# Rotated heads: swapping the halves by transfers inside SBUF in place of permutation matmuls

## The reference

```
def rope(x, pos):
    ...
    x1, x2 = xf[..., :half], xf[..., half:]
    return jnp.concatenate([x1 * cos - x2 * sin, x2 * cos + x1 * sin], axis=-1).astype(x.dtype)
```

## Time and profile before

| | |
|---|---|
| time, median of 3 runs | 2386.9 us (2386.45 to 2389.05) |
| time of the profiled execution | 2386.32 us |
| its span | 2384.5 us |
| granted TensorE clock, mean | 0.994 of full speed |
| TensorE matmul busy | 2313.1 us (97%) |
| VectorE busy | 1319.5 us (55%) |
| ScalarE busy | 954.6 us (40%) |
| GpSimd busy | 416.1 us (17%) |
| moved by DMA | 203.77 MB, mean 85 GB/s |

### The profile page before, as it was taken

One profiled execution on the slowest core, in us unless ns is written; L12 is line 12 of the kernel. 1 busy time (PEld: TensorE's weight loads), 2 busy tenths in 40 slices (PEclk: granted clock), 3 DMA queues, 4 the chain that ended last, 5 costly groups with the idle time before them and its releaser, 6 DMA issues.

```text
span 2384.5 us, 29941 instructions
## 1 busy us (share of the span) xinstructions
PE 2313.1 (97%) x11494; PEld 1821.1 (76%) x11494; DVE 1319.5 (55%) x1687; ACT 954.6 (40%) x1394; POOL 416.1 (17%) x410
## 2 busy tenths in 40 slices
PE   9999999999999989999999899999999999999997
PEld 7775668888888668888887668888888658888886
DVE  6447647664547567664548865433347685433334
ACT  4327853443323473443324353322225772323222
POOL 0003423110004134110004033200121004211000
PEclk9999999999999999999999999999999999999999
DMA  5220002222223112222223112222323201322221
GB/s 187 106 71 36 2 2 98 95 96 97 89 106 115 36 37 93 102 90 103 88 104 129 59 56 88 104 88 106 106 88 115 71 19 71 106 100 94 88 106 71
DMA packets 31493, 203.77 MB, mean 85 GB/s; under 512 B 4261, under 2 KB 5289, under 8 KB 7721
## 3 DMA queue, kind: packets, MB, share of 16 engines
q1 hardware_dynamic: 30104, 199.37, 23.5%
q10 hardware_dynamic: 1296, 3.15, 0.4%
HBM read 200.41 MB, written 2.10 MB: 85 GB/s over the span
## 4 chain that ended last, share of the span: by engine, by line
PE 84%; DVE 8%; ACT 6%; issue 2%; DMA 0%; POOL 0%; DVEq 0%; ACTq 0%; SPq 0%
PE D L586 73%; PE X L691 3%; PE D L705 3%; PE D L713 2%; DVE w_lo L1667 1%; ACT prob L1324 1%; ACT w_hi L1120 1%; ACT prob_t L1120 1%; PE X L697 1%; DVE xg L1695 1%; DVE prob L1985 1%; DVE rstd_b L1712 1%; ACT mid L1120 0%; PE X L816 0%; DVE conv_out L1805 0%
## 5 line engine op out<-in xcount | busy, mean ns | idle before, releaser
L586 PE MATMUL D<-xg,w_hi 128*128 128x512 f32 x3184 | 988.6, 392 | 6.5 <-DVE w_lo L1667 6.2
L586 PE MATMUL D<-mid,w_hi 128*128 128x512 f32 x2308 | 713.7, 390 | 16.7 <-DVE mid L1667 6.9
L586 PEld LDWEIGHTS D<-xg,w_hi 128*128 128x128 f32 x3184 | 596.3, 188 | 139.7 <-issue 9.0
L586 PE MATMUL D<-xg,w_lo 128*128 128x512 f32 x1592 | 619.7, 389 | 0.0
L1667 DVE TENSOR_TENSOR w_lo<-w_raw,w_hi 128x2048 fp32r<-128x2048 f32 (+2 forms) x210 | 458.7, 2186 | 282.0 <-ACT w_hi L1120 281.8
L1120 ACT ACTIVATE w_hi<-w_raw 128x2048 fp32r<-128x2048 f32 (+2 forms) x210 | 355.9, 1695 | 586.9 <-PE D L586 583.0
L586 PEld LDWEIGHTS D<-mid,w_hi 128*128 128x128 f32 x2308 | 433.1, 188 | 111.1 <-issue 12.1
L586 PE MATMUL D<-mid,w_lo 128*128 128x512 f32 x1154 | 449.8, 390 | 0.0
L586 PEld LDWEIGHTS D<-xg,w_lo 128*128 128x128 f32 x1592 | 298.9, 188 | 62.9
L1720 DVE TENSOR_TENSOR h<-D,h 128x1024 f32 (+1 forms) x71 | 86.9, 1224 | 354.0 <-PE D L586 353.9
L586 PEld LDWEIGHTS D<-mid,w_lo 128*128 128x128 f32 x1154 | 217.0, 188 | 45.5
(11 more groups left out here) (277 smaller groups left out, 1784.4 us busy)
## 6 DMA issues: line engine op xcount, KB each, us to landing
w_raw<-in_weights SPq DMA_DIRECT2D x184, 1024.0 KB, 4.8
h<-in_x SPq DMA_DIRECT2D x4, 512.0 KB, 7.0
out_y<-h SPq DMA_DIRECT2D x4, 512.0 KB, 2.7
w_raw<-in_weights SPq DMA_DIRECT2D x2, 512.0 KB, 6.6
inv_cnt<-in_inv_cnt ACTq DMA_DIRECT2D x1, 1024.0 KB, 5.0
cos<-in_cos ACTq DMA_DIRECT2D x3, 256.0 KB, 5.0
sin<-in_sin ACTq DMA_DIRECT2D x3, 256.0 KB, 5.4
vec<-in_vec SPq DMA_DIRECT2D x1, 272.0 KB, 2.8
```

The lines of the kernel that those rows point to most:

```text
L586: last = nc.tensor.matmul(out, w[a], x[b], start=start and k == 0, stop=stop and k == 2)
```

## The change

In nsa, swa and even the query and key tiles are no longer multiplied by the permutation. ScalarE, right behind its copy of a tile pair out of PSUM, waits until that copy is done and issues four transfers from SBUF to SBUF, each of 32 partitions, which write the swapped halves into `rope_t` (queries), `kt[:, 1]` (nsa keys, for the second pair after a wait until the first is rotated) or the new `ks2` (keys of swa and even). VectorE waits for 64 increments of `q_swapped` or `k_swapped`, and multiplies the swapped copy in place by sin; the minus sign has moved to the table of sines. `swap`, `query_swap`, `last_swap`, `swap_keys` and `swap_queries` are gone from TensorE, as are its waits that belonged to them; `key_swap` is left with the transposes of the values and is called `turn_values`. The compressed keys of nsa keep their matmul with the permutation.

```diff
+def swapped_rows():
+
+    return [(slice(r, r + HD // 2), slice(r + s, r + s + HD // 2))
+            for at in (0, HD) for r, s in ((at, HD // 2), (at + HD // 2, -(HD // 2)))]
...
+             ("ks2", [P, SEQ], F32),
...
-                    if s == 1 and kind in SINK0:
-
-                        last_swap(u)
...
-                            pe.wait_ge(q_half, late_before[l] + 1)
+                            pe.wait_ge(d_free[u % 2], u // 2 + 1)
...
-            def swap(u, out):
-
-                pe.wait_ge(d_free[u % 2], u // 2 + 1)
-                for j in range(2):
-                    last = nc.tensor.matmul(out[:, j, :], perm[:, :], zq[:, j, :], start=True, stop=True)
-                last.then_inc(q_rot, 1)
...
-            def key_swap(u, pair):
+            def turn_values(u, pair):
                 pe.wait_ge(d_free[u % 2], u // 2 + 1)
-                nc.tensor.matmul(X[:, 2 * pair, :], perm[:, :], kz2[:, :], start=True, stop=True).then_inc(k_rot, 1)
                 for t in range(QT):
                     last = nc.tensor.transpose(X[:, 2 * pair + 1, span(t)], vz2[:, span(t)], ident[:, :])
                 last.then_inc(v_turned, 1)
...
-                        if (z, k) == (0, 0):
-                            swap(u - 1, X[:, 0:2, :])
...
-                def swap_keys(n):
-                    u = at["k"] + n
-                    pe.wait_ge(d_free[u % 2], u // 2 + 1)
-                    for t in range(2):
-                        last = nc.tensor.matmul(X[:, 2 * n + t, :], perm[:, :], kz[:, n, t, :], start=True, stop=True)
-                    last.then_inc(k_rot, 1)
...
-                swap(at["q"], X[:, 0:2, :])
...
-                project(at["k"] + 1, x_norm, middle=lambda: swap_keys(0))
-                compressed_hidden(0, at["cmp_w1"], lambda: swap_keys(1))
+                project(at["k"] + 1, x_norm)
+                compressed_hidden(0, at["cmp_w1"], None)
...
-                project(at["q"] + 2, x_norm, middle=query_swap(at["q"] + 1, 0))
+                project(at["q"] + 2, x_norm)
                 project(at["gate"], x_norm, outs=1)
-                swap(at["q"] + 2, X[:, 0:2, :])
...
-                def first_middle():
-                    token_roots(l)
-                    swap(q, X[:, 0:2, :])
-
                 project(q, x_norm, norm=l)
-                project(q + 1, x_norm, middle=first_middle)
-                project(q + 2, x_norm, middle=query_swap(q + 1, 1))
+                project(q + 1, x_norm, middle=lambda: token_roots(l))
+                project(q + 2, x_norm)
                 pe.wait_ge(kv_low, 4)
-                project(at["kv"], x_kv, middle=query_swap(q + 2, 0))
-                pe.wait_ge(q_ready, qpairs_before[l] + 2)
-                project(at["q_last"], x_norm, middle=lambda: key_swap(at["kv"], 1))
+                project(at["kv"], x_kv)
+                project(at["q_last"], x_norm, middle=lambda: turn_values(at["kv"], 1))
...
-                def swap_queries():
-                    pe.wait_ge(d_free[at["pool"] % 2], at["pool"] // 2 + 1)
-                    swap(at["q"], X[:, 0:2, :])
...
-                project(at["q"], x_norm, middle=lambda: key_swap(at["kv"], 0))
+                project(at["q"], x_norm, middle=lambda: turn_values(at["kv"], 0))
...
-                project(at["q_last"], x_norm, middle=swap_queries)
+                project(at["q_last"], x_norm)
...
+                act.wait_ge(d_free[s], u // 2 + 1)
+                for out, of in swapped_rows():
+                    act.dma_start(rope_t[out, :, :], zq[of, :, :]).then_inc(q_swapped, 16)
...
+                act.wait_ge(d_free[s], u // 2 + 1)
+                for out, of in swapped_rows():
+                    act.dma_start(ks2[out, :], kz2[of, :]).then_inc(k_swapped, 16)
...
+                    if n:
+                        act.wait_ge(k_ready, krope_before[l] + n)
+                    act.wait_ge(d_free[s], (u + n) // 2 + 1)
+                    for out, of in swapped_rows():
+                        act.dma_start(kt[out, 1, :, :], kz[of, n, :, :]).then_inc(k_swapped, 16)
...
-                dve.wait_ge(q_rot, qpairs_before[l] + n + 1)
+                dve.wait_ge(q_swapped, 64 * (qpairs_before[l] + n + 1))
                 nc.vector.scalar_tensor_tensor(zq[:, :, :], zq[:, :, :], scale, cos[:, :].unsqueeze(1).to_broadcast(two),
                                                ALU.mult, ALU.mult)
-                link(nc.vector.scalar_tensor_tensor(rope_t[:, :, :], X[:, 2 * pair:2 * pair + 2, :], scale,
+                link(nc.vector.scalar_tensor_tensor(rope_t[:, :, :], rope_t[:, :, :], scale,
...
-                    dve.wait_ge(q_rot, qpairs_before[l] + n + 1)
-                    nc.vector.scalar_tensor_tensor(rope_t[:, :, :], D[:, 2 * (u % 2):2 * (u % 2) + 2, :], scale,
+                    dve.wait_ge(q_swapped, 64 * (qpairs_before[l] + n + 1))
+                    nc.vector.scalar_tensor_tensor(rope_t[:, :, :], rope_t[:, :, :], scale,
...
-            def key_rotary(l, bank):
-
-                dve.wait_ge(k_rot, krope_before[l] + 1)
-                nc.vector.tensor_tensor(rope_t[:, 0, :], kz2[:, :], cos[:, :], ALU.mult)
-                link(nc.vector.tensor_tensor(rope_t[:, 1, :], X[:, bank, :], sin[:, :], ALU.mult))
+            def key_rotary(l):
+
+                dve.wait_ge(k_swapped, 64 * (krope_before[l] + 1))
+                nc.vector.tensor_tensor(kz2[:, :], kz2[:, :], cos[:, :], ALU.mult)
+                link(nc.vector.tensor_tensor(ks2[:, :], ks2[:, :], sin[:, :], ALU.mult))
                 for g in range(2):
                     for side in range(2):
-                        ins = nc.vector.tensor_tensor(kd2[rows_of(side), g, :], rope_t[rows_of(g), 0, :],
-                                                      rope_t[rows_of(g), 1, :], ALU.add)
+                        ins = nc.vector.tensor_tensor(kd2[rows_of(side), g, :], kz2[rows_of(g), :],
+                                                      ks2[rows_of(g), :], ALU.add)
...
-                    dve.wait_ge(k_rot, krope_before[l] + n + 1)
+                    dve.wait_ge(k_swapped, 64 * (krope_before[l] + n + 1))
                     two = [P, 2, SEQ]
                     nc.vector.tensor_tensor(kt[:, 0], kz[:, n], cos[:, :].unsqueeze(1).to_broadcast(two), ALU.mult)
-                    link(nc.vector.tensor_tensor(kt[:, 1], X[:, 2 * n:2 * n + 2, :],
+                    link(nc.vector.tensor_tensor(kt[:, 1], kt[:, 1],
...
+    c["sin"] = np.where((np.arange(P) % HD < HD // 2)[:, None], -c["sin"], c["sin"])
```

More of the change, by code:

```diff
@@ L220, in build_program @@
         kdup, vall, kz, c_prob_t = (second[x] for x in ("kdup", "vall", "kz", "c_prob_t"))
-        kd2, va2, pool_s, pool_u, inv_cnt, kz2, vz2 = (
-            second[x] for x in ("kd2", "va2", "pool_s", "pool_u", "inv_cnt", "kz2", "vz2"))
+        kd2, va2, pool_s, pool_u, inv_cnt, kz2, ks2, vz2 = (
+            second[x] for x in ("kd2", "va2", "pool_s", "pool_u", "inv_cnt", "kz2", "ks2", "vz2"))
         QUERY = {"nsa": mids["q_all"], "swa": mids["q_all"], "even": mids["q_even"]}
@@ L349, in build_program @@
         out_done = sem("out_done")
[L351 removed]
+        k_swapped = sem("k_swapped")
         k_ready = sem("k_ready")
         v_ready = sem("v_ready")
[L354 removed]
+        q_swapped = sem("q_swapped")
         q_ready = sem("q_ready")
@@ L810, in attend @@
                         times_values(kind, units[n], a0 + n, n % per == per - 1)
-            def swap(u, out):
-                pe.wait_ge(d_free[u % 2], u // 2 + 1)
-                for j in range(2):
-                    last = nc.tensor.matmul(out[:, j, :], perm[:, :], zq[:, j, :], start=True, stop=True)
-                last.then_inc(q_rot, 1)
-            def query_swap(u, pair):
-                return lambda: swap(u, X[:, 2 * pair:2 * pair + 2, :])
-            def last_swap(u):
-                swap(u, D[:, 2 * (u % 2):2 * (u % 2) + 2, :])
             def attention_ends(kind, l):
@@ L889, in compressed_hidden @@
                     last.then_inc(w_used, 1)
-                    if z == 0:
+                    if z == 0 and middle is not None:
                         middle()
@@ L2119, in nsa @@
                     split_low(q + n)
-                query_rotary("nsa", l, 0, 0)
+                query_rotary("nsa", l, 0)
                 dve.wait_ge(cmp_rot, 1)
@@ L2131, in nsa @@
                 split_low(at["gate"])
-                query_rotary("nsa", l, 1, 0)
+                query_rotary("nsa", l, 1)
                 split_low(at["q_last"])
-                query_rotary("nsa", l, 2, 0)
+                query_rotary("nsa", l, 2)
                 split_low(at["v"])
@@ L2138, in nsa @@
                 split_low(at["v"] + 1)
-                query_rotary("nsa", l, 3, 0)
+                query_rotary("nsa", l, 3)
                 compressed_max(0)
@@ L2157, in swa @@
                     split_low((q + 2, at["kv"], at["q_last"])[n])
-                    query_rotary("swa", l, n, n % 2)
```

(3 more changed lines are left out.)

8 lines of the change are left out of this document (3 added, 5 removed).

## The result

| | before | after |
|---|---|---|
| time, median of 6 runs each, same chip | 2388.04 us (2386.45 to 2392.01) | 2399.07 us (2394.03 to 2404.97) |
| time of the profiled execution | 2386.32 us | 2399.79 us |
| its span | 2384.5 us | 2398.0 us |

The ratio after to before is 1.0043, 95% interval 1.0027 to 1.006. The forecast was 2384.7 us in a range of 2376 to 2393, so it was on the wrong side of no change, and the time lies beyond the range.

The account below looks back on a forecast made before the run. The prediction took TensorE, 84% of the span on the chain, as the bound. Layer changes of -5.8 (nsa), +2.35 (swa) and +1.2 us (even) sum to -2.2 on the median 2386.9, giving 2384.7 us, range 2376 to 2393.

Parts of the forecast that it names:

- the kv unit: swa's key/value projection: TensorE arrives 3.4 us earlier but waits for late weights; both swaps lost, +1.15 us.
- the late pair: Last query pair, rotated inside the attention's third step in swa: VectorE's first step starts later, +1.95 us.
- The landing term: At each swap: transfers land 2.7 us after issue, so swapped data is there 4.0 us after the copy's end.
- The transfers with slack: nsa query pairs 0, 1 and 3: later weights stay ready before TensorE needs them, so each gives 1.7 us.
- The first term: TensorE: removing 52 swap matmuls of 0.43 us takes off 22.4 us, nearly 1% if nothing else moved.
- 0.4 each, so 1.6 us: ScalarE behind each copy: four transfer issues of 0.4 us, making ScalarE 1.8 us later with wait and lost overlap.
- The second: the clock: TensorE's half speed behind pauses: nsa keys regain 2.1 us, swa's key/value projection loses 1.8; 2.74 us pauses keep full clock.
- Rival 4: Every new TensorE pause halves the clock: +2.1 us in nsa, about +1 in each attention, 2389 us; chance 0.12.
- Rival 1: ScalarE does not stand still: issues run beside its next instruction, weights never late; -12 us, 2375; chance 0.12.
- Rival 2: Transfers land late, at 5.4 us, delaying VectorE in both attentions and key rotaries; +7.6 us, 2392; chance 0.14.
- Rival 3: The four pieces of each swap serialize wholly, 10.8 us from first issue; +34 us, 2419; chance 0.04.

Follow-up runs that it names:

- nsa keys back: The changed kernel with nsa's two key swaps done by matmuls again, all other swaps by ScalarE's transfers; ratio 1.0013 to the kernel before.
- swa pairs 0, 1 back: The changed kernel with swa's first two query pairs swapped by matmuls again, everything else by ScalarE's transfers; ratio 1.0007 to the kernel before.
- the filler alone: The changed kernel plus products of bf16 zeros in TensorE's pauses in nsa and ahead of swa's key/value unit; 2393.88 us, ratio 1.0018 to the kernel before.
- issues on SyncE: The changed kernel with its 56 transfers issued by SyncE between weight loads instead of by ScalarE; 2385.91 us, ratio 0.9967 to the kernel before.
- mix 1: The kernel before with ScalarE-issued transfers only for nsa query pairs 0, 1, 3, swa pair 2 and swa's keys; 2379.19 us, ratio 0.9954.

## Why the prediction was wrong

**Read rightly.** Every place of loss was named: the nsa keys, the weights of nsa's last query unit, the kv unit, the late pair, even's last query unit. The landing term held: the late step can begin 4.2 us after the copy's end (817.34 + 1.02 to 822.55), forecast 4.0. The transfers with slack gave what was forecast: nsa's first three query copies stand at 105.06, 118.78 and 130.99 us where they stood at 102.30, 117.78 and 131.72, so 2.8 late, 1.0 late and 0.7 early, a gain of 1.7 to 1.8 for each swap between them. The first term, 22.4 us taken off TensorE, stands by the matmul count, and little of it reached the end.

**The step that failed first: "0.4 each, so 1.6 us".** It priced an issue by the earlier trace rows, loads from the device memory. An issue between partitions of SBUF took 0.61, and four of them 2.44 to 3.16 us; the hold was 2.6 to 3.1 (3.4 in even's attention), not 1.8. Where two holds stand in one chain it counts twice. That is swa's kv unit: 792.30 against 789.41, less 0.14 that was there before, is +2.75, forecast +1.15. In the nsa keys TensorE started the third unit 3.2 us late, forecast 1.3. Even's last w_lo came 2.3 us late (1.03 forecast), and its late step, behind four issues of 0.79, 3.3 instead of 1.2. The bounds of 0.35 to 0.45 were those of one group, the cosine loads, and the trace of the kernel before had dearer issues to show: the sine loads of the same line, each behind a cosine load, and the loads of the input:

```profile
L1190 ACTq DMA_DIRECT2D sin<-in_sin x3: 451/454/502, 13.0 to 1291.5; - x3
...
L552 SPq DMA_DIRECT2D h<-in_x x4: 424/520/633, 1.7 to 3.3; - x4
```

Together this step is short by 6.5 us: 1.9 in the keys, 0.9 at nsa's pair 2 (the unit behind it started at 138.96; in the kernel before it started about 138.7, worked out as the swap's start at 136.96 and its 1.72 us; the copy in front had been 0.7 early, so 1.0 was lost, forecast 0.1), 1.6 in swa and 2.1 in even.

**The second: the clock.** The forecast let the clock pay back 2.1 us in nsa and cost 1.8 in swa, nothing in the attentions, and held a pause of 2.74 us to be harmless. After, the pause of 2.57 us at 138.96 was followed by half clock (0.50 in the window above), the third compressed unit also, and swa's attention ran at half clock for 10 us behind its pause of 5, even's for 6. By the lateness ahead of each place and behind it, the term is short by 1.7 us in the keys, 1.7 at the last query unit, 0.6 at the kv unit, 2.1 in swa's attention and 3.2 in even's (1.8 behind the long pause, 1.3 later, behind one of 1.1 us at 1408.71 that kept full clock before): about 9 us. This is what is left when the waits are taken off, not a cost measured by itself, and it holds for this one execution. In "nsa keys back" and "swa pairs 0, 1 back" the same attention of even starts its late unit 2.65 us later than before and ends 3.35 later, so the clock took 0.7 there and not 3.2. Rival 4 had the mechanism, and its price of +1 in each attention was too small by half or more in this execution and about right for even in those two. That the filler alone brought back 0.25%, 6 us, agrees in kind.

So the mechanism, in which ScalarE stands still and TensorE waits at the places named, was right, and two sizes were off by 6.5 and about 9 us, which make up the 15.5 us between forecast (-2.2) and trace (+13.3). The forecast's bounds for them were 1.6 us for the issues and 2.1 for the clock. Rival 1 was wrong for this kernel; with the issues on SyncE, where ScalarE does stand free, the gain was 0.33% (8 us) against its 12. Rival 2 was wrong: of the 40 query transfers none took over 3.5 us to land. Rival 3 was wrong. The Trainium skill, page "DMA: Bandwidth & Descriptors", section "Rules for kernel authors", says of spreading transfers over several issuing engines that it does not add bandwidth and "only saves sequencer issue time". The runs agree on the second half, with 0.76% between the two issuers, and here that was the point.

What stays open: how the loss divides between issue time and clock within one layer, since a shorter hold also removes the pause that the clock answers to; and a late step whose data needs no chain of copy, issue and landing was not tried.

## What to carry to other kernels

Price a transfer by what its issuer must stop doing. Four issues of 0.61 us, 2.4 us on the engine that also writes the high parts, cost more than the matmuls that they save (four of 0.43 us for a pair, 1.72), while the same transfers issued by SyncE gain. Then move only those swaps behind which something waits with slack: five of fourteen gave 0.46%, all fourteen lost 0.43%. For each pause that an edit opens on TensorE, add the matmul time that follows it at half clock, in both directions, and treat that as the uncertain half of the sum.

## What the runs showed of the hardware

- An issue for a piece of 32 partitions inside SBUF took 0.61 us on ScalarE's queue (0.51 to 1.33), whether 128 KB or 16 KB, and 0.59 on SyncE's (0.51 to 0.64); one of 128 partitions and 512 KB took 0.47; in the kernel before, a cosine load from device memory took 0.39, a sine load 0.45, and a weight load of 1 MB on SyncE's queue 0.33. In even's attention four took 3.16 us.
- Transfers inside SBUF landed after 2.3 us (128 KB), 2.0 (64 KB), 1.8 (16 KB), 2.9 (512 KB).
- The length of a pause did not tell whether half clock (1.2 GHz) follows. The clearest case is the pause of 2.52 us in even, the same code in the kernel before and in mix 1: full clock in one, half in the other (rows above). The clock also stayed full behind 2.74 us and fell behind 2.57 us in the kernel after, and behind one of 1.08 us near the end of even's attention it stayed full before and fell after.
- Every execution also opens in its own way. TensorE's first pause, ahead of the first weights, was 0.22 us in the kernel before, and full clock followed. It was 2.17 us in mix 1, 1.91 in "issues on SyncE" and 2.05 in "swa pairs 0, 1 back", where half clock followed, and these reached nsa's first mark 2.1 to 2.2 us later. Single executions of one kernel therefore differ by some us for the clock alone, and differences of a layer below 3 us mean little without several runs.
